# Seven block products instead of eight in the second stage of twenty expert groups, and no drain of TensorE at the end of a weight chunk

## The reference

```python
def peer(xn, wq, subkeys, u, v):            # 128*128 single-neuron experts, 8 heads, 16 of them each
    ...
        e = i1 * N_KEYS + i2                # the experts chosen for a token
        g = jax.nn.softmax(c_top, axis=-1)  # their gates
        ue = jnp.take(u, e, axis=0)
        ve = jnp.take(v, e, axis=0)
        act = jax.nn.gelu(jnp.einsum('thkd,td->thk', ue, xb), approximate=False)
        return jnp.einsum('thk,thkd->td', g * act, ve)
```

## Time and profile before

| | us |
|---|---|
| median of 3 runs (2468.36 to 2478.78) | 2469.15 |
| the profiled execution | 2478.06 |
| its span | 2476.2 |
| PE busy | 2373.8 (96%) |
| DVE, ACT, POOL busy | 1319.7, 804.6, 854.2 |
| mean granted TensorE clock | 0.987 |

### The profile page before, as it was taken

One profiled execution on the slowest core, in us unless ns is written; L12 is line 12 of the kernel. 1 busy time (PEld: TensorE's weight loads), 2 busy tenths in 40 slices (PEclk: granted clock), 3 DMA queues, 4 the chain that ended last, 5 costly groups with the idle time before them and its releaser, 6 DMA issues.

```text
span 2476.2 us, 29178 instructions
## 1 busy us (share of the span) xinstructions
PE 2373.8 (96%) x11589; PEld 1184.4 (48%) x11797; DVE 1319.7 (53%) x2379; ACT 804.6 (32%) x880; POOL 854.2 (34%) x248
## 2 busy tenths in 40 slices
PE   7999999999999989999899999999999999999998
PEld 3456544444444554544565444444444444444443
DVE  2656555464425534899996555555555552222223
ACT  3232343322333433111587322222222233232321
POOL 0000345556633347420000233333333353424231
PEclk9988999999999999999999999999999999999999
DMA  6020249887852248734488966666666666666531
GB/s 209 23 80 1 102 136 237 245 253 237 250 154 69 69 129 236 214 115 152 175 319 315 318 180 179 185 187 187 187 187 187 187 196 173 192 161 194 124 79 42
DMA packets 401649, 424.98 MB, mean 172 GB/s; under 512 B 275578, under 2 KB 342270, under 8 KB 388740
## 3 DMA queue, kind: packets, MB, share of 16 engines
q1 hardware_dynamic: 395204, 411.93, 55.0%
q10 hardware_dynamic: 6336, 11.54, 1.3%
HBM read 283.97 MB, written 72.35 MB: 144 GB/s over the span
## 4 chain that ended last, share of the span: by engine, by line
PE 69%; DVE 19%; ACT 5%; POOL 2%; issue 2%; DMA 2%; DVEq 0%; SPq 0%; POOLq 0%; ACTq 0%; PEldq 0%
PE ps L1550 42%; PE ps L1817 10%; DVE arena L2492 5%; DVE arena L2499 4%; PE ps L1856 2%; DMA gate_matrix<-split 2%; PE ps L1328 2%; ACT split L1249 2%; PE ps L1643 1%; PE ps L1641 1%; ACT arena L1235 1%; PE ps L1326 1%; PE ps L1833 1%; PE ps L1301 1%; PE ps L1834 1%
## 5 line engine op out<-in xcount | busy, mean ns | idle before, releaser
L1550 PE MATMUL ps<-split,arena 128*128 128x512 bf16 x4232 | 936.7, 380 | 21.0 <-DVE x_sb L2514 9.0
L1550 PEld LDWEIGHTS ps<-split,arena 128*128 128x128 bf16 x4320 | 420.9, 98 | 533.0 <-DVE x_sb L2514 14.4
L868 POOL TENSOR_TENSOR split<-ring,split 128x4096 bf16<-128x4096 f32 x32 | 259.3, 8102 | 891.3 <-ACT split L1249 891.3
L1817 PE MATMUL ps<-arena 128*128 128x512 bf16 x1881 | 415.5, 380 | 2.0
L2514 DVE TENSOR_TENSOR x_sb<-ps,x_sb 128x512 f32<-128x512 f32 x256 | 173.8, 690 | 323.1 <-PE ps L1550 323.1
L2492 DVE TENSOR_TENSOR arena<-arena 128x512 f32<-128x512 f32 x128 | 179.6, 1403 | 238.7 <-ACT arena L1242 142.1
L1550 PE MATMUL ps<-arena,split 128*128 128x512 bf16 x1314 | 292.3, 380 | 7.2 <-PE ps L1550 4.2
L1817 PEld LDWEIGHTS ps<-arena 128*128 128x128 bf16 x1920 | 187.7, 98 | 226.7
L772 POOL TENSOR_TENSOR split<-ring,split 128x4096 bf16<-128x4096 f32 x26 | 207.2, 7970 | 220.5 <-ACT split L1039 218.1
L1550 PEld LDWEIGHTS ps<-arena,split 128*128 128x128 bf16 x1344 | 142.6, 107 | 151.5 <-issue 7.7
L2499 DVE TENSOR_TENSOR arena<-arena 128x512 bf16<-128x512 f32 x128 | 157.3, 1229 | 67.3 <-ACT arena L1235 33.7
(11 more groups left out here) (305 smaller groups left out, 2406.2 us busy)
## 6 DMA issues: line engine op xcount, KB each, us to landing
ring<-in_peer_v SPq DMA_DIRECT2D x32, 2048.0 KB, 7.8
ring<-in_peer_u SPq DMA_DIRECT2D x20, 2048.0 KB, 8.4
ring<-in_w_ff SPq DMA_DIRECT2D x16, 2048.0 KB, 8.5
gate_matrix<-split SPq DMA_DIRECT2D x16, 2048.0 KB, 8.3
arena<-gate_matrix SPq DMA_DIRECT2D x32, 1024.0 KB, 8.4
arena<-in_peer_u SPq DMA_DIRECT2D x48, 512.0 KB, 4.8
turned_table<-u_split SPq DMA_DIRECT2D x48, 512.0 KB, 5.5
ring<-turned_table SPq DMA_DIRECT2D x12, 2048.0 KB, 9.3
```

The costliest lines, as they stand in the source:

```text
L868: pool.tensor_tensor(split[:, s2, 1, :], ring[:, slot, :], split[:, s2, 0, :], ALU.subtract).then_inc(w_lo, 1)
L1550: mm = pe.matmul(dst, a(k), b(k), start=n == 0, stop=n == len(terms) - 1)
L1817: mm = pe.matmul(up_bank(j), a, b, start=n == 0, stop=n == len(terms) - 1)
```

## The change

- The second stage of twenty live groups (order numbers 1, 3, ..., 19, 21, then 22 to 30) is computed by a scheme with seven products of half-size blocks instead of eight (Winograd's form of Strassen's): 14 outputs of 6 matmuls, 84 matmuls instead of 96.
- For that, POOL builds four sums of blocks of v in the ring buffer, and v is split in seven pieces of 1024 columns, each with a copy on ACT and a subtraction on POOL. u's low part is made in four pieces of 1024.
- The hidden values' sums are built in PSUM: ACT's gelu works in place, DVE multiplies in place, ACT copies, DVE does five 256-column steps for a pair of tiles.
- The seven products go into accumulators that are kept over all groups; 16 DVE additions at the end combine them into the output.
- The stored groups' second stage stays as it was, with `v` split in two halves. Part of the hidden values' room is now the room of `gelu_back`, so `load_gelu(i+1)` waits for the live group's low parts, and SP issues it later in its order.
- `w_used` is gone. ACT waits on PE's output counters instead.

The core of the diff:

```diff
@@ sync
             for i in range(EARLY):
                 g = EARLY + i
                 sp.wait_ge(ex_mul, 4 * (2 * i) + 4)
-                if i + 1 < EARLY:
-                    load_gelu(i + 1)
                 load_gates(2 * i + 2)
-                sp.wait_ge(w_lo, S_EX + 2 * i + 1)
+                sp.wait_ge(w_lo, S_EX + 2 * i + 2)
                 load_v(2 * i + 2)
...
                 sp.wait_ge(u_split_lo, i + 1)
                 load_u(g + 3)
                 for half in range(2):
                     if i >= 1:
                         sp.wait_ge(ex_a, 4 * g + (2 * half + 2))
                     turn_rows(half)
-                if i >= 1:
-                    sp.wait_ge(w_lo, S_EX + 2 * i + 2)
-                    load_v(2 * i + 3)
-                    sp.wait_ge(ex_mul, 4 * (2 * i + 1) + 4)
-                    load_gates(2 * i + 3)
+                sp.wait_ge(ex_mul, 4 * (2 * i + 1) + 4)
+                load_gates(2 * i + 3)
+                if i < EARLY - 1:
+                    sp.wait_ge(part_lo_done, 2 * i + 2)
+                    load_gelu(i + 1)
+                    sp.wait_ge(v_lo, 7 * i + 7)
+                    load_v(2 * i + 3)
@@ gpsimd
+            half_lows(0)
+            for i in range(EARLY):
+                first_blocks(i, 1)
+                if i >= 1:
+                    half_lows(i)
                 u_low(EARLY + 1 + i, u_place(EARLY + 1 + i)[0])
-                v_low(2 * i + 1, 1, 0)
+                last_blocks(i, 1)
@@ scalar
             for i in range(EARLY):
+                g, s = EARLY + i, 2 * i + 1
+                if i >= 1:
+                    down_summed(act, s - 3)
+                for j in range(4):
+                    stored_tile(i, j)
+                first_blocks(i, *v_place(s), s - 2 if i >= 1 else None)
+                if i >= 1:
+                    half_highs(i)
+                live_gelu(g, 0)
+                u_high(g + 1, *u_place(g + 1))
+                live_gelu(g, 1)
...
@@ tensor
-                pe.wait_ge(mm_done, done_before + 4)
-                pe.sem_inc(w_used, 1)
...
+            def down_bank_free(s, n):
+                pe.wait_ge(ex_add, outputs(s) + (n + 1))
...
+            def seven_down(s, l, buf, first_bank):
+                pe.wait_ge(part_lo_done, 2 * l + 2)
+                for i, q in enumerate((0, 6, 1, 4, 5, 3, 2)):
+                    pe.wait_ge(v_lo, 7 * l + (1, 3, 3, 4, 5, 6, 7)[i])
+                    for r in range(2):
+                        rows_ = slice(r * P, (r + 1) * P)
+                        down_bank_free(s, 2 * i + r)
+                        three_pass(down_bank(first_bank + 2 * i + r), lambda j: part_hi[buf][:, q, j, rows_], lambda j: part_lo[buf][:, q, j, rows_],
+                                   lambda j: part_place(i, 0)[:, j, :], lambda j: part_place(i, 1)[:, j, :], 2).then_inc(ex_b, 1)
@@ vector
             def stored_hidden(i):
                 s = 2 * i
                 dve.wait_ge(gates_in[0], 16 * (i + 1))
                 dve.wait_ge(gelu_in, 16 * (i + 1))
-                group_summed(dve, s)
+                past = [] if i == 0 else list(range(14))
                 for j in range(4):
                     gate_times(gelu_back[:, j, :], 0, j)
-                    if i >= 1:
-                        add_one(s - 1, 2 * j)
-                    low_part(s, 0, j)
-                    if i >= 1:
-                        add_one(s - 1, 2 * j + 1)
+                    for n in past[0:2]:
+                        add_part(s - 1, n, outputs(s - 1))
+                    dve.wait_ge(whole_hi_done, 4 * i + j + 1)
+                    dve.tensor_tensor(whole_lo[:, j, :], gelu_back[:, j, :], whole_hi[:, j, :], ALU.subtract).then_inc(whole_lo_done, 1)
+                    for n in past[2:4]:
+                        add_part(s - 1, n, outputs(s - 1))
+                    past = past[4:]
+            def live_hidden(g, s, l, buf, par, copy, gate_loads, add, count):
+                dve.wait_ge(gates_in[par], gate_loads)
+                part_gelu(s, g, par, 0)
+                part_gelu(s, g, par, 1)
+                part_lows(l, buf, 0)
+                part_adds(l, 0, copy)
+                part_sums_lows(l, buf, 0)
+                part_gelu(s, g, par, 2)
+                part_gelu(s, g, par, 3)
+                add(0)
+                part_lows(l, buf, 1)
+                add(1)
+                part_adds(l, 1, copy)
+                add(2)
+                add(3)
+                part_sums_lows(l, buf, 1)
+                for n in range(4, count):
+                    add(n)
```

More of the change, by code:

```diff
@@ L1076, in _ @@
             with act.Fori(0, 3) as i:
+                act.wait_ge(ff_a, 4)
+                act.wait_ge(ff_b, 16 * i + 1)
                 split_high(4 * i + 4, 0, i + 2)
@@ new lines, in block_high, with first_blocks @@
+            def block_high(i, block):
+                act.activation(part_place(i, 0), block, ACT.Copy).then_inc(v_hi, 1)
+            def first_blocks(l, slot, rounds, past, between=None):
+                b11, b12, b21, b22 = (v_block(slot, e, c) for e in range(2) for c in range(2))
+                act.wait_ge(ring_in[slot], arrived(slot, rounds))
+                if past is not None:
+                    product_summed(act, past, 0)
+                block_high(0, b11)
+                if between is not None:
+                    between()
+                if past is not None:
+                    product_summed(act, past, 2)
+                block_high(2, b21)
+                act.wait_ge(v_sums, 4 * l + 1)
+                block_high(1, b11)
+                if past is not None:
+                    product_summed(act, past, 3)
+                act.wait_ge(v_sums, 4 * l + 2)
+                block_high(3, b12)
@@ L1291, in _ @@
+            slot, rounds = v_place(31)
+            act.wait_ge(ring_in[slot], arrived(slot, rounds))
+            for half in range(2):
+                act.wait_ge(u_across[half], 32 * (EX_GROUPS - EARLY - 1))
+            act.activation(u_split[:, 0, :], ring[:, slot, :], ACT.Copy).then_inc(w_hi, 1)
             for t in range(NT):
-                act.wait_ge(ex_add, 8 * (EX_GROUPS - 1) + 2 * t + 6)
+                act.wait_ge(ex_add, outputs(EX_GROUPS - 1) + 2 * t + 6)
                 sum_squares(x_sb[:, t, :], ps[:, 6:8, :].rearrange("p a b -> p (a b)"), t)
@@ new lines, in _, with add_to, products_out @@
+            for n in range(14):
+                add_part(30, n, outputs(30))
+            def add_to(dst, src):
+                own.wait()
+                own.did(dve.tensor_tensor(dst, dst, src, ALU.add))
+            def products_out(r):
+                dve.wait_ge(ex_add, outputs(EX_GROUPS - 1) + 4)
+                add_to(sums_6[r], sums_1[r])
+                add_to(x_sb[:, r, 0:512], sums_1[r])
+                add_to(sums_7[r], sums_6[r])
+                add_to(x_sb[:, r, 512:1024], sums_6[r])
+                add_to(x_sb[:, 2 + r, 0:512], sums_7[r])
+                add_to(x_sb[:, 2 + r, 512:1024], sums_7[r])
+                add_to(x_sb[:, r, 512:1024], sums_5[r])
+                add_to(x_sb[:, 2 + r, 512:1024], sums_5[r])
```

444 lines of the change are left out of this document (295 added, 149 removed).

## The result

The changed kernel takes 2576.13 us in the median of four runs (2574.03 to 2578.03), the kernel before 2469.31 (2468.36 to 2478.78): the ratio is 1.0404, 95% interval 1.0381 to 1.0427. It is 107 us slower; 62 had been forecast. Between the two profiled executions it is 2575.43 against 2478.06, 97.4 us; the other 9 are those by which the profiled execution of before lies above its median. The times of nearly every kernel here come at two levels some 10 us apart (before at about 2469 and 2479), so medians can differ by that alone.

The account below looks back on a forecast made before the run. TensorE was taken to bound before, and after it a loop of waits through POOL, SP and DMA in stored-group rounds. +86.4 - 12 - 12.4 = +62 gave 2531 against the median, forecast 2532 us, range 2510 to 2560.

Parts of the forecast that it names:

- the wider one: Range for the whole time, 2485 to 2575 us, leaving out the first two rivals and a tail above.
- Matmuls removed: Twenty second stages lose 12 matmuls each, 2.59 us a stage, 51.8 us in all if TensorE stays the bound.
- Drains: TensorE's 18 waits for itself at weight chunks' ends go, 0.69 us each: 12.4 us less, bounds -12.4 and 0.
- The loop: Rounds with a stored group wait through DVE, TensorE, ACT, POOL, SP's queue and the landing: at least 68.3 us each.
- The clock: After each gap in those rounds TensorE runs about 6 us at half speed: 3 us a round, bounds 0 and 4.
- The first landing: First arrival of stored activations in the expert rounds, put at 1418.8 us by adding ACT, POOL, queue and transfer times.
- The late rounds: Ten later second stages save 25.9 us; DVE's late third addition takes back 0.9 each, 9 in all; together -12.
- The pattern change: Between rounds with a stored group and later ones, SP's order makes the first loads late: 5 us lost.
- The sum: Whole profiled execution: +86.4 for stored-group rounds, -12 for later rounds, -12.4 for drains, giving +62.
- TensorE stays the bound: Rival: the load lands before 59.6 us of its loop, so the kernel gets faster, 2419 us; chance 0.07.
- POOL becomes the bound of both halves: Rival: slow small POOL pieces add 36 us in the loop and 10 in late rounds, 2575 us; chance 0.13.

Follow-up runs that it names:

- The best version: Changed kernel with the loads of stored activations and live v issued earlier, DVE's first wait and ACT's seventh-piece copy moved later: 2423.29 us median, ratio 0.9783.
- The first two experiments: Changed kernel, separately: stored activations' load moved right behind u's load, 2478.9 us; 44 unused matmuls added ahead of the fifth output in ten stages, 2558.44 us.
- the run without sums: Changed kernel with POOL's four sums of blocks of v left out for each group, results then wrong: 2509.91 us.
- the late load in the kernel before: Kernel before with only the stored activations' load moved behind u, the transposes and the second gate load: 2484.03 us, ratio 1.0046.
- the better one: Changed kernel with the stored activations' load right behind u's load and live v's load between the transpose pairs: 2442.71 us.
- the last two experiments: Changed kernel without POOL's sums of v, 2509.91 us; the 2424.0 us kernel with ACT's seventh-piece copy behind the first hidden copies, 2423.29 us.
- the version with 2424.0 us: Changed kernel with stored activations' load behind u's, live v's between transpose pairs, and DVE's wait for all 44 stored activations ahead of round two: 2424.0 us.

## Why the prediction was right, and where it was short

It forecast slower with 0.87, by this loop; both stand. The size was 44 us short: 2576.13 lies above its range from 2510 to 2560, and by 1 us above the wider one that ends at 2575.

- **Matmuls removed**: right as TensorE's work. The best version has the rounds of 59.57 and 38.85 us that were worked out.
- **Drains**: the mechanism is right (alone, 9 us less, nothing in its place), the size is not: 12.4 was 18 times the 0.69 of one chunk. The row of all 18 sums to 9.1, and the second stage of the first round began 8.3 us sooner in the changed kernel (1372.22 against 1380.56). The sum was in the row and should have been taken from it.
- **The loop**: right. The first two experiments, the run without sums and the late load in the kernel before show its parts: last to land is the stored activations' load; POOL is in it piece by piece; neither the late place nor TensorE's idle time alone makes it. TensorE's gap in it is 11.3 us in the mean (101.7 in nine), where 7 to 10 had been said. Predicted round 71.3, measured (2078.60 - 1420.67) / 9 = 73.1, where landings are meant. In the round shown, ACT's first piece ends at 17.8 (14.9 and 3 for the clock predicted), u's low part 30.2 later (29.4: a float32 result costs 2.35 to 2.68, not 2.10), SP's queue is 16.5 (15.5), the landing 8.8 (8.5). Nine rounds of 1.8 make 16 us. (ACT's ten pieces at 1.05 are 10.5, not 8.4; the chain passes only the first, so nothing came of it.)
- **The clock**: the mechanism is right, the size too high. It is at 0.50 when work resumes in nine rounds of nine, but full 2.7 to 5.7 us later, 4.3 in the mean (after the landing shown above, work from 1569.18, full from 1573.2), where the one gap of the earlier trace rows had given 6. Half of 4.3 is 2.2 us, and filling the gap gives back 2.0 a round; 3 had been taken, out of 0 to 4. This term was 1 us a round too high, and the other parts of the loop too low by that and the 1.8 of the round. The Trainium skill (TensorE: Matmul & The Clock Gate, HAM oscillation) has this as paid again at every step; the trace agrees, in nine rounds of nine.
- **The first landing**: this is the step that failed most. The prediction had it at 1418.8 - 12.4 = 1406.4, it was 1420.67, +14. The start was taken to move ahead with the drains. But DVE's first gate products stand behind a new wait, for the last store of all 44 early activations (10.88 us of DMA from 1352.33, and 32.6 us of waiting in DVE's row). It is a line of the new code ahead of the loop, which the prediction never priced. Moved, it gave 8.7 us in the changed kernel and 8 in the better one; with it gone, v is next. Of the 14.3, 3.3 are the drains' (9.1 for 12.4); 8.0 more lie ahead of POOL's first piece (1371.64), 6.2 of which went with the wait and 1.8 are v's own landing; 2.3 are SP's queue, 17.8 here (1394.13 to 1411.97) for 15.5; and 0.6 are POOL and the transfer.
- **The late rounds**: the stall was forecast at 0.9 and is 1.06, for the wrong reason. It was put on DVE's order, the third addition behind the five steps; the last two experiments show that these start late because ACT stands behind POOL's last sum. POOL is 72% busy there (301.41 of 420 us), and its share said nothing of it. The pattern change costs a wait of 2.9 us for u's transposes, a slower first stage after it (22.45 instead of 20.88), and waits of 3.1 and 1.0 in the next group, 8.5 instead of 5. Without POOL's sums all of this is gone. Eight groups lose 1.39 each over their matmuls, 11.1 instead of 9. Together that is 5.6 more than forecast; this part came out 5.2 above it.
- **The sum** of the misses on the profiled execution (first landing, rounds, from the last landing to the next second stage, the rest): 14.3 + 16.2 - 0.3 + 5.2 = 35.4, and 62 + 35.4 is the 97.4 measured. The other 9 of the 107 are the level: the forecast took them off with the median of before, and the runs of after stayed at the upper one.
- **The rivals**: *TensorE stays the bound* was priced at 2419 and is near what the best version does (2413 and 2423), once the landings are early enough; that the numbers meet is in part chance, since 2419 took 12.4 for the drains and had 9 for a late stall that this version doesn't have. *POOL becomes the bound of both halves* had the number nearest to the result (2575; its own terms, 36 and 10 on 2532, give 2578) and half its mechanism: its pieces take 2.13, under the 2.2 it asked for, but the sums 2.35 to 2.68, and in the late part it does set a wait, through ACT. The time came out there mostly by other causes, so that its number was near is luck.

## What to carry to other kernels

Follow what a change adds to the instructions ahead of each transfer's issue, and who is queued behind its landing: together they can close a loop through TensorE, the three elementwise engines and the transfers, and the loop then runs at the sum of its parts. Busy shares don't show it: from 1400 to 1960 us TensorE was busy 84% of the time, POOL 55%, DVE 43% and ACT 31%. Read every wait that the new code adds before its loops, not only those within. When a wait's releaser is named, ask what released that engine in turn: DVE's late addition was ACT's late copy was POOL's last sum, and the cure was one moved line.

## What the runs showed of the hardware

A landing's price goes with what is in the queue ahead: 1 MB of stored activations took 5.0 us behind nothing and 8.7 behind transposes and gates.

DVE's longest operations shrank with POOL's pieces. Before, DVE operations with both inputs in SBUF took up to 8437 ns beside POOL's instructions of 8 us; after, the gate products of this kind take 693 at most and the low parts 2460. Line 2492 before, then line 2694 after (count, ns min/median/max):

```profile
L2492 DVE TENSOR_TENSOR arena<-arena x78: 680/684/8437, 1403.3 to 2008.7; 128x512 f32<-128x512 f32 x78
```

```profile
L2694 DVE TENSOR_TENSOR arena<-arena x40: 678/681/693, 1420.8 to 2093.8; 128x512 f32<-128x512 f32 x40
```

In the kernel before, TensorE's work hid these but for its waits of 0.8 us a round. The Trainium skill (SBUF — State Buffer, Who interferes with whom) says that a `tensor_tensor` with both inputs in SBUF contends with GpSimd's reads; the trace agrees, and the longest time goes with the length of POOL's instruction. The order on both engines changed as well, and no run changes the size of the pieces alone.

The granted clock fell in the loop's gaps of 11 to 12 us: 0.50 at their end in nine of nine, and full 2.7 to 5.7 us after work resumed. In the late groups it stayed at 1.00 through the waits of 1.0 and 3.1 us; after one of 4.5 us (in the version with 2424.0 us, up to 2058.13) it was 0.67 and 0.65 in the next 5 us.

The two levels, 10 us apart, go with one difference of the granted clock between 100 and 200 us (0.83 to 0.85 in seven of the profiled executions, 0.94 to 0.97 in the other four). What decides which one an execution gets no run here shows.
